# Stationary pieces of a routed-expert layer moved to seven other places in SBUF relative to the weights

## The chip, the cores and the metric

The kernel runs on one core of a Trainium2 chip. The metric is the device time of one execution in microseconds (us). Three executions of the kernel before took 2636.76, 2640.47 and 2642.72 us; the median is 2640.47 us.

The core has a matrix engine (PE in the profile), which takes a stationary operand (128 columns, loaded by LDWEIGHTS, shown as PEld) and streams a moving operand past it (MATMUL); a vector engine (DVE), a scalar engine (ACT), GpSimd (POOL) and SyncE (SP), which issues most of the transfers. SBUF is the on-chip memory: 128 partitions, in each of which a tile takes one range of byte addresses.

## The reference

One transformer-like layer in float32 over 2048 tokens of width 1024. Cut to what the change touches:

```python
y_lru = (h_f + h_b) * gelu(ga)                       # 512 columns, recurrent branch
y_ret = head_rms(o).reshape(B, T, 512) * silu(g)     # 512 columns, retention branch
x = x + g1 * (concatenate([y_lru, y_ret]) @ w_out)   # output projection
h = modulate(rmsnorm(x), sh2, sc2)
s = sigmoid(h @ w_router); eidx, gates = top 6 of 64 experts, by groups
routed = sum over a token's 6 experts of gate * (silu(h @ w1[e]) * (h @ w3[e])) @ w2[e]
x = x + g2 * (routed + shared expert)                # expert width 256
out = rmsnorm(x)
```

## The kernel before, in words

Float32 products run on PE in a reduced format (`F32R`), in three passes: each operand is split into a high part and the low remainder, and a product is high x high, high x low and low x high. The weights are always the moving operand, 512 columns at a time; the activations are the stationary operand, in pieces of 128 columns (512 bytes per partition). Both lie in SBUF. So each MATMUL of a product is preceded by a LDWEIGHTS of a 512-byte piece, and reads 2048 bytes of weights per partition.

The program has four stages, one after the other: `front` (input projection, scans, chunk states), `mixer_out` (retention output, output projection L1745, router, lists of tokens per expert), `experts` (shared expert in 16 blocks of 128 tokens, then 136 blocks of routed tokens, two to a loop turn), and `final` (last norm).

In `mixer_out`, `out_products` (L1745) multiplies four stationary tiles with the output weights: `yl_hi`, `yl_lo`, `y_ret_t_hi`, `y_ret_t_lo`.

In `experts`, `step` on PE does for one block k: 16 matmuls with `x_t[0]` (tile `x_exp_t_hi`; 8 pieces against the high weights and again against the low ones, into `ps_h`), two transposes of the block before (`ps_ht`), 8 matmuls with `x_t[1]` (`x_exp_t_lo`), 8 transposes of the gathered rows for the next block (`ps_x`), and `down` for the block before: for each half of 512 output columns, 4 matmuls with `h_t[0]` (`h_exp_t_hi`) and 2 with `h_t[1]` (`h_exp_t_lo`) into `ps_y`. That is 40 product matmuls and 10 transposes. The helper `products` issues all the product matmuls of this stage at L2429. Blocks alternate between two halves (`par` 0 and 1) of `x_t` and `h_t`. ACT writes the high parts (L2205, L2196, L2211), DVE the low parts (L2261, L2267); ACT (L2182, L2186) and DVE (L2247, L2252) split each expert's weights from the raw ring `w_exp` into the tile called `shared` once per expert, POOL gathers token rows (L2135) and adds the results back to memory (L2145), and SP loads raw expert weights. The order of each engine's work is written out by hand and held together by semaphores; it does not depend on where tiles lie.

Two smaller products of `mixer_out` serve as comparisons below: `ps_o` at L1814 takes the same stationary tile `qf_t` (256 modulo 512) against `sf_ctx` (128 modulo 512) in one `par` and against `sf_m` (256) in the other. Of tiles that transfers read or write, `shared_raw` and `xt` begin at 0 modulo 64, `kvqg_out` and `xa_ga_out` at 32.

Tiles are placed one behind the other in the order in which they are allocated, each rounded up to 32 bytes. In the built program the split weights (the tile `shared`) begin at byte 19200 of every partition, which is 256 modulo 512, and every 512-column block of them is a multiple of 2048 bytes further. Before the change every stationary tile of a product also begins at 256 modulo 512 (`x_exp_t_hi` at 208640, `x_exp_t_lo` at 216832, `h_exp_t_hi` at 225024, `yl_hi` at 188160, `y_ret_t_hi` at 212736), and its pieces lie 512 bytes apart: the distance from stationary to weights is 0 modulo 512 throughout.

Of the kernel before, what the change touches and what calls it, by code (L numbers as in the profile page):

```python
# [19 lines left out]
F32R = mybir.dt.float32r  # L20
# [1389 lines left out]
def mixer_out(nc, for_dma, io, mod_d, hx_d, rec_d, yl_d, h2_d, h2t_d, sum_d, list_d, sf, ident, gc, Z, early, R, pre, pre_loaded):  # L1410
# [4 lines left out]
    with ExitStack() as ctx:  # L1415
        def sb(name, shape, dt=F32):
            return ctx.enter_context(nc.sbuf_tensor(name, shape, dt))
# [17 lines left out]
        rec = Z.rec  # L1435
        x = sb("x_m", [P, 2, D])
        yl_raw = sb("yl_m", [P, 2, NCT * P])
        yl = [sb("yl_hi", [P, 2, NCT * P]), sb("yl_lo", [P, 2, NCT * P])]
        q_t = sb("q_t", [P, HD])
        qf_t = sb("qf_t", [P, HD])  # L1440
        qb_t = sb("qb_t", [P, HD])
# [2 lines left out]
        sfd = sb("sf_decayed", [P, HD])  # L1444
        sq_o = sb("sq_out_o", [P, HEADS, DH])
        y = sb("y_ret", [P, HD])
        y_t = [sb("y_ret_t_hi", [P, HD]), sb("y_ret_t_lo", [P, HD])]
        x1, h2 = Z.x1, Z.h2
        sq_x = sb("sq_out_x", [P, D])
        gain = sq_x  # L1450
# [457 lines left out]
    return out  # L1908


def experts(nc, for_dma, io, mod_d, h2_d, h2t_d, sum_d, list_d, ident, Z, R, pre, pre_loaded, blocks_row, ends_row):

# [8 lines left out]
    N_GU, N_D = WE // CHUNK, WD // CHUNK  # L1921
    STAGES = WE // D
    FIRST_SPLIT = NT - 4
    with ExitStack() as ctx:
        def sb(name, shape, dt=F32):
            return ctx.enter_context(nc.sbuf_tensor(name, shape, dt))
# [10 lines left out]
        w_raw = sb("w_exp", [P, RING * W])  # L1937
        w = Z.w_exp
        g2, gate, who = Z.g2, Z.gate, Z.who.bitcast(U32)
        block_row = sb("block_rows", [P, 2], U32)  # L1940
        take = sb("take", [P, 2], U32)

        lists = R.eq6[:].rearrange("p b j e -> p (b j e)")[:, 0:4 * P].rearrange("p (c t w) -> p c t w", c=2, w=2)
        xg, y = pre[:, 0:2], pre[:, 2:4]
        x_t = [sb("x_exp_t_hi", [P, 2, KC * P]), sb("x_exp_t_lo", [P, 2, KC * P])]
        th, hg = Z.th, Z.hg
        h_t = [sb("h_exp_t_hi", [P, 2, D_EXP]), sb("h_exp_t_lo", [P, 2, D_EXP])]
        nt, nti, end, ones = Z.nt, Z.nti.bitcast(I32), Z.end, Z.ones
# [6 lines left out]
        give = sb("give", [P, 2], U32)  # L1955
        kc = sb("size_key_col", [P, 1])
        ncol = sb("nt_col", [P, 1])
        rnk = sb("size_rank", [P, 1])
        er, de = Z.er, Z.de
        ecol = sb("expert_cols", [P, 2])  # L1960
        bcol = sb("block_cols", [P, 2, 2])
        scol = sb("start_cols", [P, 2])
# [216 lines left out]
        def _(act):  # L2179
# [8 lines left out]
            def copy_shared(k, par):  # L2188
                if k == 0:
                    act.wait_ge(pre_loaded, 32)  # L2190
                else:
                    act.wait_ge(xs_loaded[k % STAGES], (k // STAGES + (k % STAGES > 0)) * 16)
                wait(act, h_done, k - 1)
                for b in range(2):
                    c = slice(b * 512, (b + 1) * 512)
                    act.activation(x_t[0][:, par, c].bitcast(F32R), stage(k)[:, c], ACT.Copy).then_inc(xt_hi, 1)  # L2196

            def copy_xt(k, par):
                if isinstance(k, int) and k < NT:
                    copy_shared(k, par)  # L2200
                    return
                wait(act, h_done, k - 1)
                for b in range(2):
                    act.wait_ge(xt_done, (k - NT) * 2 + 1 + b)
                    act.activation(x_t[0][:, par, b * 512:(b + 1) * 512].bitcast(F32R), ps_x[:, b],  # L2205
                                   ACT.Copy).then_inc(xt_hi, 1)

            def copy_ht(k, par):
# [33 lines left out]
        def _(dve):  # L2242
# [12 lines left out]
            def copy_xt(k, par):  # L2255
                wait(dve, h_done, k - 1)
                for b in range(2):
                    c = slice(b * 512, (b + 1) * 512)
                    dve.wait_ge(xt_hi, k * 2 + 1 + b)
                    src = stage(k)[:, c] if isinstance(k, int) and k < NT else ps_x[:, b]  # L2260
                    dve.tensor_tensor(x_t[1][:, par, c].bitcast(F32R), src, x_t[0][:, par, c],  # L2261
                                      ALU.subtract).then_inc(xt_lo, 1)

            def copy_ht(k, par):
# [51 lines left out]
            def sizes(tabs):  # L2316


                dve.wait_ge(R.carry_done, NT)
                dve.wait_ge(gu_hi, N_GU)  # L2320
                dve.wait_ge(rows_done, 1)
                tabs.of(dve.scalar_tensor_tensor(nt[:, 1:NE], R.iota[:], -float(LIST), R.carry[:], ALU.mult, ALU.add))
                tabs.of(dve.tensor_scalar(nti[:], nt[:, 1:NE], float(P - 1 - LIST), None, ALU.add))
                tabs.of(dve.tensor_scalar(nti[:], nti[:], 7, None, ALU.arith_shift_right))
                tabs.of(dve.tensor_copy(nt[:, 1:NE], nti[:]))
                tabs.of(dve.tensor_scalar(nt[:, 1:NE], nt[:, 1:NE], 1.0, None, ALU.max))
                tabs.of(dve.scalar_tensor_tensor(key[:], nt[:, 1:NE], float(N_EXP), R.iota[:], ALU.mult, ALU.subtract))
# [3 lines left out]
                tabs.of(dve.tensor_reduce(ncol[:], own_key[:], AX.X, ALU.add))
                tabs.of(dve.tensor_scalar(own_key[:], key[:], kc[:], None, ALU.is_gt))
                tabs.of(dve.tensor_reduce(rnk[:], own_key[:], AX.X, ALU.add))
                dve.tensor_scalar(by_size[:, 0], R.rank_at[:], rnk[:], ncol[:], ALU.is_equal, ALU.mult).then_inc(sized, 1)
                dve.tensor_scalar(by_size[:, 1], R.rank_at[:], rnk[:], R.kcol[:, 2:3], ALU.is_equal, ALU.mult).then_inc(sized, 1)
# [80 lines left out]
        def _(pe):  # L2416
# [39 lines left out]
            def step(k, par, r):  # L2456
# [4 lines left out]
                pe.wait_ge(gu_hi, (e + 1) * N_GU)  # L2461
                pe.wait_ge(xt_hi, (k + 1) * 2)
                wait(pe, hg_done, k - 1)
                products(ps_h[:, par], x_t[0][:, par], w[0], at, KC, 512, start=True)
                pe.wait_ge(gu_lo, (e + 1) * N_GU)
                products(ps_h[:, par], x_t[0][:, par], w[1], at, KC, 512)
# [3 lines left out]
                products(ps_h[:, par], x_t[1][:, par], w[0], at, KC, 512, stop=True).then_inc(h_done, 1)  # L2470
# [100 lines left out]
def build(nc, io, out):  # L2571
# [16 lines left out]
    with ExitStack() as for_dma, ExitStack() as ctx:  # L2588
# [6 lines left out]
        early = for_dma.enter_context(nc.semaphore("rec_loaded0"))  # L2595
        front(nc, for_dma, io, mod_d, hx_d, xa_d, ga_d, kr_d, rec_d, yl_d, h2_d, sum_d, list_d, sf, ident, gc, Z, early)
        blocks_row = Z.blocks_row
        ends_row = ctx.enter_context(nc.sbuf_tensor("ends_row", [1, NE + 1], I32))
        with ExitStack() as routing:
            R = Routing(nc, routing, for_dma)  # L2600
            pre = routing.enter_context(nc.sbuf_tensor("w_shared_raw", [P, 4, D], F32))
            pre_loaded = for_dma.enter_context(nc.semaphore("pre_loaded"))
            mixer_out(nc, for_dma, io, mod_d, hx_d, rec_d, yl_d, h2_d, h2t_d, sum_d, list_d, sf, ident, gc, Z, early, R, pre, pre_loaded)
            experts(nc, for_dma, io, mod_d, h2_d, h2t_d, sum_d, list_d, ident, Z, R, pre, pre_loaded, blocks_row, ends_row)
        final(nc, for_dma, io, sum_d, out)


# [14 lines left out]
```

## Time and profile before

| | |
|---|---|
| median of three executions | 2640.47 us (2636.76 to 2642.72) |
| the profiled execution's own time | 2637.47 us |
| its span, first to last instruction | 2635.7 us |
| PE busy | 2461.7 us, 93% of the span |
| PE weight loads busy | 2011.9 us, 76% |
| DVE, ACT, POOL busy | 1717.1, 1012.1, 988.2 us |
| mean granted PE clock | 0.97 of 2.4 GHz |
| product matmuls of `experts` (L2429) | 2432 + 1216 + 1216 + 608 = 5472 of 11959 PE instructions |

The duration of one MATMUL in the profile includes the time for its result to leave the array, which overlaps the next one. What a matmul costs in a dense run is the distance from one start to the next. A merged line of the timeline gives it: the line's length, less the length of one instruction, over the count less one.

### The profile page before, as it was taken

The page shows a single profiled execution, that of the slowest core. Times are in us where ns is not written, and L with a number is a line of the kernel's source. Part 1 is how long each engine was busy: PE and PEld are TensorE (multiplying, and loading weights), DVE is VectorE, ACT ScalarE, POOL GpSimd, SP SyncE. Part 2 cuts the span into 40 slices and gives each one's busy share as a digit, 9 for nine tenths or more (in the row PEclk, how much of TensorE's full clock was granted, in tenths as well). Part 3 has the DMA queues.
Part 4 walks back from the last instruction along what each step waited for, and adds up shares of the span by engine and source line. Part 5 has one row for each costly group of instructions (what it writes and reads, how often), then busy time and mean ns, then how long its engine had stood idle before and what let it go on. Part 6 is the DMA issues. An engine that isn't in the chain of part 4 may idle for free. (4 is left out here: it accounts for less than half of the span.)

```text
span 2635.7 us, 47416 instructions
## 1 busy us (share of the span) xinstructions
PE 2461.7 (93%) x11959; PEld 2011.9 (76%) x11960; DVE 1717.1 (65%) x2741; ACT 1012.1 (38%) x1619; POOL 988.2 (37%) x1009
## 2 busy tenths in 40 slices
PE   7999999998989999889999999999999999999990
PEld 4788777776767888668888887887888888888870
DVE  4663674557345666765567768587876768778673
ACT  2321433333432222222334445354554535445442
POOL 1211016542153677741233333333333433434344
PEclk8999999999989999989999999999999999999995
DMA  7775676756766556346869979899997989979887
GB/s 295 280 284 219 233 274 243 273 210 231 282 240 236 195 188 199 126 133 167 247 169 268 282 209 304 220 301 280 286 315 193 278 256 302 292 215 307 258 239 279
DMA packets 240999, 646.32 MB, mean 245 GB/s; under 512 B 24205, under 2 KB 37841, under 8 KB 224913
## 3 DMA queue, kind: packets, MB, share of 16 engines
q1 hardware_dynamic: 190480, 463.95, 49.1%
q0 software_dynamic: 50432, 181.27, 27.5%
q8 instruction: 48, 0.79, 0.1%
q14 instruction: 39, 0.31, 0.0%
HBM read 467.81 MB, written 177.33 MB: 245 GB/s over the span
## 5 line engine op out<-in xcount | busy, mean ns | idle before, releaser
L2429 PE MATMUL ps_h<-shared,x_exp_t_hi 128*128 (+1 forms) x2432 | 580.0, 391 | 7.4 <-ACT x_exp_t_hi L2196 7.4
L2429 PEld LDWEIGHTS ps_h<-shared,x_exp_t_hi 128*128 128x128 f32 x2432 | 457.2, 188 | 104.5 <-issue 9.1
L2145 POOL DMA_INDIRECT sum_d<-w_shared_raw,give x136 | 236.7, 1740 | 612.1 <-DMA sum_d<-w_shared_raw,give 276.5
L1216 PE MATMUL ps_p<-shared 128*128 128x512 f32 x1632 | 392.5, 399 | 6.5 <-DVE kvqg_out L105 3.3
L1216 PEld LDWEIGHTS ps_p<-shared 128*128 128x128 f32 x1632 | 308.5, 190 | 75.9 <-DVE kvqg_out L105 4.1
L2429 PE MATMUL ps_y<-shared,h_exp_t_hi 128*128 (+1 forms) x1216 | 342.4, 404 | 19.0 <-DVE h_exp_t_lo L2267 14.7
L2429 PE MATMUL ps_h<-shared,x_exp_t_lo 128*128 (+1 forms) x1216 | 318.6, 404 | 0.0
L2247 DVE TENSOR_TENSOR shared<-w_exp,shared (+1 forms) x256 | 307.0, 1220 | 10.0 <-ACT shared L2182 4.7
L2211 ACT ACTIVATE h_exp_t_hi<-ps_ht 128x256 fp32r<-128x256 f32 x152 | 58.4, 384 | 615.5 <-PE ps_ht L2438 613.3
L2429 PEld LDWEIGHTS ps_y<-shared,h_exp_t_hi 128*128 128x128 f32 x1216 | 220.1, 190 | 62.3 <-issue 22.0
L2182 ACT ACTIVATE shared<-w_exp (+1 forms) x256 | 255.4, 1056 | 22.5 <-DMA w_exp<-in_experts 19.5
L2429 PEld LDWEIGHTS ps_h<-shared,x_exp_t_lo 128*128 128x128 f32 x1216 | 216.9, 188 | 39.2
L2289 DVE SCALAR_TENSOR_TENSOR w_shared_raw<-ps_y,shared_raw 128x512 f32<-128x512 f32 x272 | 191.4, 745 | 81.4 <-PE ps_y L2429 59.3
L2429 PE MATMUL ps_y<-shared,h_exp_t_lo 128*128 (+1 forms) x608 | 189.6, 393 | 0.0
L2135 POOL DMA_INDIRECT w_shared_raw<-h_d,take x139 | 147.9, 1064 | 108.8 <-POOL take L2133 105.9
L2261 DVE TENSOR_TENSOR x_exp_t_lo<-ps_x,x_exp_t_hi 128x512 fp32r<-128x512 f32 x274 | 175.6, 682 | 0.0
L2305 DVE SCALAR_TENSOR_TENSOR shared_raw<-shared_raw,ps_h 128x256 f32<-128x256 f32 x152 | 63.8, 420 | 147.8 <-ACT shared_raw L2216 137.9
L2267 DVE TENSOR_TENSOR h_exp_t_lo<-ps_ht,h_exp_t_hi 128x256 fp32r<-128x256 f32 x152 | 64.2, 422 | 141.0 <-ACT h_exp_t_hi L2211 138.2
L2252 DVE TENSOR_TENSOR shared<-w_exp,shared (+1 forms) x130 | 153.1, 1219 | 2.0 <-ACT shared L2186 2.0
L2205 ACT ACTIVATE x_exp_t_hi<-ps_x 128x512 fp32r<-128x512 f32 x274 | 148.1, 594 | 2.2
L2423 PEld LDWEIGHTS ps_x<-ident,w_shared_raw 128*128 128x128 f32 x1096 | 128.1, 141 | 18.6
L2423 PE MATMUL ps_x<-ident,w_shared_raw 128*128 128x128 f32 x1096 | 141.9, 272 | 0.0
(296 smaller groups left out, 3601.8 us busy)
## 6 DMA issues: line engine op xcount, KB each, us to landing
w_exp<-in_experts SPq DMA_DIRECT2D x386, 512.0 KB
shared<-hx_d SPq DMA_DIRECT2D x58, 1024.0 KB, 7.1
shared<-rec_d SPq DMA_DIRECT2D x16, 1536.0 KB
shared_raw<-in_w_mod_rest POOLq DMA_DIRECT2D x16, 1024.0 KB, 5.7
rec_d<-shared_raw SPq DMA_DIRECT2D x48, 256.0 KB, 5.0
rec_d<-kvqg_out SPq DMA_DIRECT2D x48, 256.0 KB, 4.6
hx_d<-shared SPq DMA_DIRECT2D x10, 1024.0 KB, 5.8
xt<-in_xt POOLq DMA_DIRECT2D x18, 512.0 KB, 8.3
```

What stands on the lines that cost most here:

```text
L1216: last = pe.matmul(ps_p[:, s % 2], hx0[:, at, x, k].bitcast(F32R), wa[w][:, k, p % 2 * HD:(p % 2 + 1) * HD].bitcast(F32R), start=(m + k == ...
L2135: pool.indirect_dma_start(xg[:, par], None, h2_d[:, :], bass.IndirectOffsetOnAxis(take[:, par:par + 1], 0)).then_inc(gathered[par], 16)
L2145: pool.indirect_dma_start(sum_d[:, :], bass.IndirectOffsetOnAxis(give[:, par:par + 1], 0), y[:, par], None, compute_op=ALU.add).then_inc(a ...
L2182: act.activation(w[0][:, piece(e, i)].bitcast(F32R), raw(e, i), ACT.Copy).then_inc(gu_hi, 1)
L2205: act.activation(x_t[0][:, par, b * 512:(b + 1) * 512].bitcast(F32R), ps_x[:, b], ACT.Copy).then_inc(xt_hi, 1)
L2247: dve.tensor_tensor(w[1][:, piece(e, i)].bitcast(F32R), raw(e, i), w[0][:, piece(e, i)], ALU.subtract).then_inc(gu_lo, 1)
L2252: dve.tensor_tensor(w[1][:, piece(e, i)].bitcast(F32R), raw(e, i), w[0][:, piece(e, i)], ALU.subtract).then_inc(wd_lo, 1)
L2261: dve.tensor_tensor(x_t[1][:, par, c].bitcast(F32R), src, x_t[0][:, par, c], ALU.subtract).then_inc(xt_lo, 1)
L2267: dve.tensor_tensor(h_t[1][:, par].bitcast(F32R), ps_t[:, 0:D_EXP], h_t[0][:, par], ALU.subtract).then_inc(ht_lo, 1)
L2289: dve.scalar_tensor_tensor(y[:, par, c], ps_y[:, i], gate[:, bass.ds(k, 1)], g2[:, c], ALU.mult, ALU.mult).then_inc(y_done, 1)
L2423: last = pe.transpose(ps_x[:, b, j * P:(j + 1) * P], xg[:, par, c:c + P], ident[:])
L2429: last = pe.matmul(out, x[:, j * P:(j + 1) * P].bitcast(F32R), w_part[:, bass.ds(w_at + j * stride, 512)].bitcast(F32R), start=(start and ...
```

## The change

It moves tiles and changes nothing else: the 10522 instructions of the built program stand in the same order on every engine with the same operations and waits; only addresses differ.

- `experts`: `x_exp_t_hi` and `x_exp_t_lo` are cut into a tile for each `par`, with 128 unused bytes between them. Modulo 512 they begin at 0, 128, 256 and 384. `h_exp_t_hi` and `h_exp_t_lo` begin at 384. Room for this comes from packing the small column tiles into one (`small_cols`) and putting `ends_row` into an idle part of `R.prod`.
- `mixer_out`: unused tiles (`apart_m0` to `apart_m3`) put `yl_hi` at 192 and `yl_lo` at 224 modulo 512; `y_ret_t_hi` begins at 272 and `y_ret_t_lo` at 264.
- Since `ends_row` is gone, everything allocated behind it begins 288 bytes earlier: the raw ring `w_exp` at 159136 instead of 159424 (32 instead of 0 modulo 64), the rows that are gathered and scattered (`w_shared_raw`) at 142752 instead of 143040.

| stationary tile | distance from the weights before | after | matmuls |
|---|---|---|---|
| `x_exp_t_hi`, par 0 | 0 | 256 | 1216 |
| `x_exp_t_hi`, par 1 | 0 | 384 | 1216 |
| `x_exp_t_lo`, par 0 | 0 | 0 | 608 |
| `x_exp_t_lo`, par 1 | 0 | 128 | 608 |
| `h_exp_t_hi` and `_lo` | 0 | 128 | 1216 + 608 |
| `yl_hi` | 0 | 448 | 256 |
| `yl_lo` | 0 | 480 | 128 |
| `y_ret_t_hi` | 0 | 16 | 256 |
| `y_ret_t_lo` | 0 | 8 | 128 |

(distance modulo 512 bytes, stationary less weights)

```diff
@@ mixer_out
-        yl = [sb("yl_hi", [P, 2, NCT * P]), sb("yl_lo", [P, 2, NCT * P])]
+        sb("apart_m0", [P, 56])
+        yl_hi_t = sb("yl_hi", [P, 2, NCT * P])
+        sb("apart_m1", [P, 8])
+        yl = [yl_hi_t, sb("yl_lo", [P, 2, NCT * P])]
...
-        y_t = [sb("y_ret_t_hi", [P, HD]), sb("y_ret_t_lo", [P, HD])]
+        sb("apart_m2", [P, 8])
+        y_t_hi = sb("y_ret_t_hi_at", [P, HD + 4])
+        sb("apart_m3", [P, 120])
+        y_t_lo = sb("y_ret_t_lo_at", [P, HD + 2])
+        y_t = [y_t_hi[:, 4:], y_t_lo[:, 2:]]
@@ experts
+    ENDS_AT = 2 * N_EXP + 2 * NE + 6
...
-        block_row = sb("block_rows", [P, 2], U32)
-        take = sb("take", [P, 2], U32)
+        small = sb("small_cols", [P, 24])
+        block_row, take, give = (small[:, i:i + 2].bitcast(U32) for i in (0, 2, 4))
+        kc, ncol, rnk = (small[:, i:i + 1] for i in (6, 7, 8))
+        ecol, scol = small[:, 9:11], small[:, 11:13]
+        bcol = small[:, 13:17].rearrange("p (c j) -> p c j", c=2)
...
-        x_t = [sb("x_exp_t_hi", [P, 2, KC * P]), sb("x_exp_t_lo", [P, 2, KC * P])]
+        x_t_hi = [sb("x_exp_t_hi0", [P, KC * P])]
+        sb("apart_hi", [P, 32])
+        x_t_hi.append(sb("x_exp_t_hi1", [P, KC * P]))
+        sb("apart_hi_lo", [P, 32])
+        x_t_lo = [sb("x_exp_t_lo0", [P, KC * P])]
+        sb("apart_lo", [P, 32])
+        x_t_lo.append(sb("x_exp_t_lo1", [P, KC * P]))
+        x_t = [x_t_hi, x_t_lo]
...
+        ends_row = R.prod[:].rearrange("p j e -> p (j e)")[0:1, ENDS_AT:ENDS_AT + NE + 1].bitcast(I32)
...
-                products(ps_h[:, par], x_t[0][:, par], w[0], at, KC, 512, start=True)
+                products(ps_h[:, par], x_t[0][par], w[0], at, KC, 512, start=True)
@@ build
-        ends_row = ctx.enter_context(nc.sbuf_tensor("ends_row", [1, NE + 1], I32))
```

## Rows read from the trace of the kernel before

**Rows 1.** The page, busy time of each engine with share and instructions.
```profile
PE 2461.7 (93%) x11959; PEld 2011.9 (76%) x11960; DVE 1717.1 (65%) x2741; ACT 1012.1 (38%) x1619; POOL 988.2 (37%) x1009
```

**Rows 2.** Windows: stretch, its length, busy time of each engine, PE clock, DMA share, GB/s.
```profile
960.00:1150.00 190.00, 160.89 (x933) 138.37 (x932) 132.01 (x423) 50.21 (x139) 131.11 (x131) 0.93 0.49 165
1300.00:1600.00 300.00, 300.00 (x1480) 249.68 (x1479) 206.65 (x299) 126.65 (x200) 107.43 (x128) 1.00 0.83 240
2200.00:2540.00 340.00, 336.76 (x1657) 279.25 (x1656) 260.69 (x362) 168.36 (x252) 133.10 (x144) 1.00 0.93 282
```

**Rows 3.** Waits, 1150 to 2540 us: who waited for whom, us, times, longest.
```profile
PE ps_y L2429 <- DVE h_exp_t_lo L2267: 10.9, 11, 2.2
ACT shared L2182 <- DMA w_exp<-in_experts: 19.5, 14, 3.6
```

**Rows 4.** Timeline of PE, one expert block: start, length (us), instruction, count.
```profile
1503.85 3.79 PE L2429 MATMUL ps_h<-shared,x_exp_t_hi 128*128 x16
1507.48 0.38 PE L2438 MATMUL ps_ht<-ident,shared_raw 128*128 128x128 f32 x2
1507.62 2.10 PE L2429 MATMUL ps_h<-shared,x_exp_t_lo 128*128 x8
1509.56 1.03 PE L2423 MATMUL ps_x<-ident,w_shared_raw 128*128 128x128 f32 x8
1511.82 1.07 PE L2429 MATMUL ps_y<-shared,h_exp_t_hi 128*128 x4
1513.18 2.20 PE L2429 MATMUL ps_h<-shared,x_exp_t_hi 128*128 x9
```

**Rows 5.** Timeline of PE, first five and last six of those sixteen matmuls.
```profile
1503.85 1.30 PE L2429 MATMUL ps_h<-shared,x_exp_t_hi 128*128 x5
...
1506.12 1.53 PE L2429 MATMUL ps_h<-shared,x_exp_t_hi 128*128 x6
```

**Rows 6.** Line L1745, 815 to 836 us: duration ns min/median/max, starts, form.
```profile
L1745 PE MATMUL ps_u<-shared,y_ret_t_hi x16: 389/389/389, 822.5 to 826.8; 128*128 128x512 f32 x16
```

**Rows 7.** Timeline of PE, output projection in the mixer.
```profile
822.49 1.98 PE L1745 MATMUL ps_u<-shared,y_ret_t_hi 128*128 128x512 f32 x8
```

**Rows 8.** The context states' products: timeline, then durations of line L1238.
```profile
494.34 1.89 PE L1238 MATMUL ps_kt_kv<-shared_raw 128*128 128x256 f32 x8
...
L1238 PE MATMUL ps_kt_kv<-shared_raw x8: 377/379/379, 494.3 to 495.9; 128*128 128x256 f32 x8
```

**Rows 9.** Timeline of PE, retention output with either state tile.
```profile
947.69 0.39 PE L1813 MATMUL ps_o<-shared,scores_t 128*128 128x128 f32 x2
947.91 0.39 PE L1814 MATMUL ps_o<-sf_ctx,qf_t 128*128 128x128 f32 x2
948.13 0.39 PE L1815 MATMUL ps_o<-shared,qb_t 128*128 128x128 f32 x2
...
967.78 0.39 PE L1813 MATMUL ps_o<-shared,scores_t 128*128 128x128 f32 x2
968.00 0.39 PE L1814 MATMUL ps_o<-sf_m,qf_t 128*128 128x128 f32 x2
968.23 0.39 PE L1815 MATMUL ps_o<-shared,qb_t 128*128 128x128 f32 x2
```

**Rows 10.** DMA issues: count, KB each, median us from issue to landing.
```profile
rec_d<-shared_raw SPq DMA_DIRECT2D x48, 256.0 KB, 5.0
rec_d<-kvqg_out SPq DMA_DIRECT2D x48, 256.0 KB, 4.6
xa_ga_out<-in_w_mod_head SPq DMA_DIRECT2D x2, 1024.0 KB, 11.1
xt<-in_w_mod_head SPq DMA_DIRECT2D x2, 1024.0 KB, 12.1
```

**Rows 11.** Instruction groups of ACT and DVE: count, busy us, mean ns, idle before.
```profile
L2205 ACT ACTIVATE x_exp_t_hi<-ps_x 128x512 fp32r<-128x512 f32 x274 | 148.1, 594 | 2.2
L2261 DVE TENSOR_TENSOR x_exp_t_lo<-ps_x,x_exp_t_hi 128x512 fp32r<-128x512 f32 x274 | 175.6, 682 | 0.0
```

More of the change, by code:

```diff
@@ L1908, in constants, with experts @@
     return out
-def experts(nc, for_dma, io, mod_d, h2_d, h2t_d, sum_d, list_d, ident, Z, R, pre, pre_loaded, blocks_row, ends_row):
+def experts(nc, for_dma, io, mod_d, h2_d, h2t_d, sum_d, list_d, ident, Z, R, pre, pre_loaded, blocks_row):
     RING = 2
@@ L1954, in experts @@
         cmpe = room[:, 2 * N_EXP:2 * N_EXP + 2 * NE].rearrange("p (c e) -> p c e", c=2)
[L1955 to L1958, printed above, removed]
         er, de = Z.er, Z.de
-        ecol = sb("expert_cols", [P, 2])
-        bcol = sb("block_cols", [P, 2, 2])
-        scol = sb("start_cols", [P, 2])
+        ends_row = R.prod[:].rearrange("p j e -> p (j e)")[0:1, ENDS_AT:ENDS_AT + NE + 1].bitcast(I32)
         ps_h = ctx.enter_context(nc.psum_tensor("ps_h", [P, 2, 512], F32))
@@ L2195, in copy_shared @@
                     c = slice(b * 512, (b + 1) * 512)
-                    act.activation(x_t[0][:, par, c].bitcast(F32R), stage(k)[:, c], ACT.Copy).then_inc(xt_hi, 1)
+                    act.activation(x_t[0][par][:, c].bitcast(F32R), stage(k)[:, c], ACT.Copy).then_inc(xt_hi, 1)
             def copy_xt(k, par):
@@ L2204, in copy_xt @@
                     act.wait_ge(xt_done, (k - NT) * 2 + 1 + b)
-                    act.activation(x_t[0][:, par, b * 512:(b + 1) * 512].bitcast(F32R), ps_x[:, b],
+                    act.activation(x_t[0][par][:, b * 512:(b + 1) * 512].bitcast(F32R), ps_x[:, b],
                                    ACT.Copy).then_inc(xt_hi, 1)
@@ L2260, in copy_xt @@
                     src = stage(k)[:, c] if isinstance(k, int) and k < NT else ps_x[:, b]
-                    dve.tensor_tensor(x_t[1][:, par, c].bitcast(F32R), src, x_t[0][:, par, c],
+                    dve.tensor_tensor(x_t[1][par][:, c].bitcast(F32R), src, x_t[0][par][:, c],
                                       ALU.subtract).then_inc(xt_lo, 1)
@@ L2328, in sizes @@
                 tabs.of(dve.tensor_tensor(own_key[:], key[:], ident[:, 0:N_EXP], ALU.mult))
-                tabs.of(dve.tensor_reduce(kc[:], own_key[:], AX.X, ALU.add))
+                tabs.of(dve.tensor_reduce(kc, own_key[:], AX.X, ALU.add))
                 tabs.of(dve.tensor_tensor(own_key[:], nt[:, 1:NE], ident[:, 0:N_EXP], ALU.mult))
[L2331 to L2335, printed above, removed]
+                tabs.of(dve.tensor_reduce(ncol, own_key[:], AX.X, ALU.add))
+                tabs.of(dve.tensor_scalar(own_key[:], key[:], kc, None, ALU.is_gt))
+                tabs.of(dve.tensor_reduce(rnk, own_key[:], AX.X, ALU.add))
+                dve.tensor_scalar(by_size[:, 0], R.rank_at[:], rnk, ncol, ALU.is_equal, ALU.mult).then_inc(sized, 1)
+                dve.tensor_scalar(by_size[:, 1], R.rank_at[:], rnk, R.kcol[:, 2:3], ALU.is_equal, ALU.mult).then_inc(sized, 1)
             def counts(tabs):
@@ L2463, in step @@
                 wait(pe, hg_done, k - 1)
-                products(ps_h[:, par], x_t[0][:, par], w[0], at, KC, 512, start=True)
+                products(ps_h[:, par], x_t[0][par], w[0], at, KC, 512, start=True)
                 pe.wait_ge(gu_lo, (e + 1) * N_GU)
-                products(ps_h[:, par], x_t[0][:, par], w[1], at, KC, 512)
+                products(ps_h[:, par], x_t[0][par], w[1], at, KC, 512)
                 if not isinstance(k, int) or k > 0:
@@ L2469, in step @@
                 pe.wait_ge(xt_lo, (k + 1) * 2)
-                products(ps_h[:, par], x_t[1][:, par], w[0], at, KC, 512, stop=True).then_inc(h_done, 1)
+                products(ps_h[:, par], x_t[1][par], w[0], at, KC, 512, stop=True).then_inc(h_done, 1)
                 if not isinstance(k, int) or k >= NT - 1:
@@ L2603, in build @@
             mixer_out(nc, for_dma, io, mod_d, hx_d, rec_d, yl_d, h2_d, h2t_d, sum_d, list_d, sf, ident, gc, Z, early, R, pre, pre_loaded)
-            experts(nc, for_dma, io, mod_d, h2_d, h2t_d, sum_d, list_d, ident, Z, R, pre, pre_loaded, blocks_row, ends_row)
+            experts(nc, for_dma, io, mod_d, h2_d, h2t_d, sum_d, list_d, ident, Z, R, pre, pre_loaded, blocks_row)
         final(nc, for_dma, io, sum_d, out)
```

## Prediction, made before the changed kernel was run

> **What bounds the kernel now.** I read the page first: PE is busy 93% of the span, DVE 65%, the others less than half [rows 1]. A share over the whole program hides stages with different limits, so I took the windows next. From 1300 to 1600 us, inside the routed experts, PE is busy 300.0 of 300 us at full clock, and from 2200 to 2540 us 336.8 of 340, while DVE has 206.7 and 260.7 there; only the mixer's second half is looser, 160.9 of 190 [rows 2]. The waits from 1150 to 2540 us agree: the largest wait of PE is 10.9 us in total, and the raw expert weights, which ACT awaits for 19.5 us in all, never appear as what held PE up [rows 3]. So in the experts the time is the sum of the matmul spacings, and a nanosecond more or less on each product matmul comes straight out at the end. The change touches exactly that and nothing else: the order of instructions is the same, so no wait, no transfer and no queue position is added or removed.
>
> **What one product matmul costs now.** One block runs from 1503.85 to 1513.18 us, 9.33 us [rows 4]; 152 blocks of that length are 1418 us. In it, sixteen matmuls with the high part of x take (3.79 - 0.389) / 15 = 0.2267 us each, 0.389 being the length of a single undisturbed one [rows 4, 6]. Transposes take (1.03 - 0.27) / 7 = 0.109 each [rows 4]. The two transposes and the eight low-part matmuls behind them last 1509.56 - 1507.48 = 2.08 us; less 2 x 0.109 that is 1.862 / 8 = 0.2328 us a matmul, so a product run behind transposes is dearer than a clean one, by 6.1 ns each [rows 4]. In the mixer the clean rate is the same, (1.98 - 0.389) / 7 = 0.2273 [rows 6, 7]. And there is a stream without the surcharge: the eight float32 products of the context states take (1.89 - 0.379) / 7 = 0.2159 us each, although a 128 x 128 load stands before each of them too [rows 8]. They stream 256 columns in the time in which a product streams 512, so they read SBUF at half the pace. From 0.2159 to 0.2267 are 10.8 ns a matmul: something about reading 512 columns at the doubled pace beside a load costs that. Whether it depends on where the two operands lie is the whole question.
>
> **The change part by part.** Moved relative to the weights are, by the instruction counts, 2432 matmuls with the high part of x (half to distance 256, half to 384), 608 of the 1216 with the low part (to 128), 1824 with the two parts of h (to 128), and in the mixer 256 (448), 128 (480), 256 (16) and 128 (8): 4864 in the experts and 768 in the mixer, 5632 together. 608 with the low part of x stay at distance 0.
>
> No row of before has a full-pace product at another distance modulo 512, so the cost of the move has to be bounded. Below: at best each moved matmul loses the whole surcharge, -10.8 ns x 5632 = -61 us [rows 4, 8]. Above: the nearest dearer rate is the disturbed one, +6.1 ns x 5632 = +34 us [rows 4]. I take 0, for three reasons.
>
> First, the distance does change within one run today, in larger steps, and nothing happens. Pieces lie 512 bytes apart and their weight blocks 2048, so over the eight pieces the distance passes through 0, 512, 1024 and 1536 modulo 2048. The first five matmuls of the run take (1.30 - 0.389) / 4 = 0.228 and the last six (1.53 - 0.389) / 5 = 0.228 [rows 5]. Even the middle is uniform, or the length of the sixteen would not fit. So no address bit above 512 bytes matters.
>
> Second, arithmetic on the two readers. A load passes 512 bytes of a partition in the 0.109 us that a transpose with its load takes [rows 4], while the stream of 2048 bytes in 0.2267 us passes about 1000. The stream therefore moves at twice the load's pace, and during one load the difference of the two addresses runs once through 512 bytes whatever it was at the start. If memory were divided in banks that repeat within 512 bytes, each load would meet the stream as often from any starting distance, only in another order. This is inference, not a reading, and it does not exclude that the order matters.
>
> Third, the nearest comparison at another distance. The retention output uses stationary `qf_t` with `sf_ctx` at distance 128 and with `sf_m` at distance 0. Two matmuls with either take the same step: 948.13 - 947.91 = 0.22 and 968.23 - 968.00 = 0.23 us [rows 9]. These are float32 and load-bound, so the witness is weak, but it points to nothing.
>
> For the mixer's four places the same value, 0, with 768 x (-10.8 to +6.1 ns) = -8.3 to +4.7 us inside the bounds above. A distance of 8 bytes is the only one that is not a multiple of 16, and it has 128 matmuls: at 6.1 ns 0.8 us.
>
> The Trainium skill has a rule on this: "SBUF — State Buffer", section "Who interferes with whom", gives PE two independent read ports, one for the moving operand and one for the loads, and says that PE never waits on anyone. By that rule place cannot matter and the sum would be 0, as forecast; but this trace disagrees with its plainest reading, since 0.2267 against 0.2159 us is a surcharge that a wholly free second port would not leave [rows 4, 8].
>
> Two side effects. Everything allocated behind the removed `ends_row` starts 288 bytes earlier, which moves the raw weight ring and the gathered rows from 0 to 32 modulo 64. Transfers to and from such tiles exist today: stores of 256 KB land in 5.0 us from a tile at 0 and in 4.6 from one at 32, loads of 1024 KB in 12.1 and 11.1 us [rows 10]. So 0, and the cover that hides a small loss is the 19.5 us that ACT, not PE, waits for these loads [rows 3]. The copies that fill the stationary tiles, 594 ns on ACT and 682 ns on DVE, keep their shapes; even 10% on each of the pair would be 0.13 us per tile half in a block of 9.33 us, hidden while DVE has a quarter of its time free [rows 2, 11]. Packing the small columns changes addresses of single-column operands only: 0.
>
> The sum is 0. Against the profiled execution's 2637.5 us that gives 2637.5; the median of the three executions is 3 us above it, and I forecast against that: 2640 us.
>
> **The rivals.**
> *Slower: some of the new distances collide more.* Runs behind transposes show that a product matmul can cost 0.2328 instead of 0.2267 at distance 0, so the surcharge depends on how load and stream stand to each other in time [rows 4]; a shift in address can act like a shift in time, and my second reason says nothing on order. If all expert places settle at the dearer rate: 6.1 ns x 4864 = +30 us, 2670. If only the most used, distance 128, does (608 + 1824 = 2432 matmuls): +15 us, 2655. It decides from 1 ns on 5632 matmuls, 5.6 us, upward. Against it stand the even rate over eight pieces and the retention pair [rows 5, 9].
> *Faster: the surcharge is a conflict of equal places.* At distance 0 load and stream start in the same residue; a start half a period away might avoid the meeting. All of the experts' matmuls freed: -10.8 x 4864 = -53 us, 2588; only distance 256 freed: 1216 x 10.8 = -13 us, 2627. DVE would still fit (260.7 us of work in 340 - 12 or so) [rows 2]. The skill's "TensorE: Matmul & The Clock Gate", section "Back-to-back issue gap", gives about 216 ns for 512 columns at full clock, which is the price a freed matmul would have; the trace shows it only in the half-pace stream [rows 8]. Against it: the even rate over four distances modulo 2048.
> *Slower by transfers: the ring at 32 modulo 64.* Slower loads would lengthen ACT's waits first and PE's only at the changes of expert. There are 64 of those; an uncovered 0.1 us at each is 6 us, 2646, and that is the point from which it decides. The landings speak against it [rows 10].
>
> **How the numbers follow.** Two medians of this kernel can be told apart at about 0.2%, 5.3 us. No measurable change: 0.60. Slower by address: 0.19; slower by transfers: 0.03. Faster by address: 0.18. The no-change case alone spans 2635 to 2646. The range goes on to 2660 above (the one-place case at 2655 inside, all places at 2670 outside, about 0.07) and to 2622 below (one freed place at 2627 inside, more outside, about 0.09), which leaves out some 0.16 to 0.2. Faster 0.18, same 0.60, slower 0.22.
>
> **What the changed profile would show.** If I am right, the run of sixteen `ps_h` matmuls is 3.79 us long in both halves of the loop, the single matmul 389 ns, and the eight behind the transposes end 2.08 us after the transposes begin, alike with the moved low part (par 1) and the unmoved one (par 0). The low part gives a control inside one trace: if par 1 and par 0 differ, place matters. The mixer's `y_ret_t_hi` run stays 1.98 us. I am wrong if runs of sixteen differ from 3.79 us by more than 0.02 us (1 ns each), or if they are equal and PE instead shows new waits on ACT or DVE at a change of expert.

## The result: 16 us slower, and the profile after

| | before | after |
|---|---|---|
| median (range) of four executions each, us | 2640.29 (2636.76 to 2642.72) | 2656.73 (2654.84 to 2659.96) |
| ratio, with its 95% interval | | 1.0061 [1.0048, 1.0074] |
| span of the profiled execution | 2635.7 | 2655.9 |
| front, up to the mixer | 778.4 | 776.6 |
| mixer | 356.7 | 360.8 |
| shared expert, 16 blocks | 144.9 | 146.7 |
| routed experts, 136 blocks | 1293.2 | 1309.3 |
| final norm | 62.5 | 62.6 |

The stages are worked out from the starts of PE's instructions in the two traces. The experts carry the change, with a smaller part in the mixer. The page's busy line of the changed kernel, beside [rows 1]:

```profile
PE 2478.9 (93%) x11959; PEld 2015.3 (76%) x11960; DVE 1723.3 (65%) x2741; ACT 1011.1 (38%) x1619; POOL 988.7 (37%) x1009
```

PE is busy 17.2 us longer with the same 11959 instructions. The windows of the changed kernel, in the stretches and columns of [rows 2]:

```profile
960.00:1150.00 190.00, 158.50 (x914) 135.48 (x913) 132.07 (x411) 49.84 (x138) 126.20 (x129) 0.93 0.49 162
1300.00:1600.00 300.00, 300.00 (x1465) 247.60 (x1464) 205.59 (x296) 125.33 (x200) 108.26 (x127) 1.00 0.83 236
2200.00:2540.00 340.00, 335.47 (x1625) 276.03 (x1624) 259.73 (x358) 167.29 (x250) 126.92 (x141) 0.99 0.91 274
```

From 1300 to 1600 us PE is as full as before and at the same clock, but gets through 1465 instructions instead of 1480: each takes longer, nothing is waited for. The waits, 1150 to 2560 us, beside [rows 3]:

```profile
ACT shared L2194 <- DMA w_exp<-in_experts: 30.4, 17, 4.0
...
PE ps_y L2441 <- DVE h_exp_t_lo L2279: 14.6, 13, 2.2
```

ACT's wait for raw weights grew by 11 us, and PE's largest by 3.7. PE's belongs to the changes of expert, and what these cost varies from run to run: blocks longer than 9.7 us were 12, with 15.1 us above 9.35 each, before; 13 with 21.6 us after; and 12 with 20.3 us in a kernel below whose time is that of before. I don't count it to the change.

The timeline of PE in one loop turn (two blocks), start, length, instruction, count, answers to [rows 4]. The block at 1500.64 is par 1, the one at 1510.11 par 0:

```profile
1500.64 3.88 PE L2441 MATMUL ps_h<-shared,x_exp_t_hi 128*128 x16
1504.36 0.38 PE L2450 MATMUL ps_ht<-ident,shared_raw 128*128 128x128 f32 x2
1504.50 2.11 PE L2441 MATMUL ps_h<-shared,x_exp_t_lo 128*128 x8
1506.45 1.04 PE L2435 MATMUL ps_x<-ident,w_shared_raw 128*128 128x128 f32 x8
...
1508.71 1.10 PE L2441 MATMUL ps_y<-shared,h_exp_t_hi 128*128 x4
...
1510.11 3.80 PE L2441 MATMUL ps_h<-shared,x_exp_t_hi 128*128 x16
1513.75 0.38 PE L2450 MATMUL ps_ht<-ident,shared_raw 128*128 128x128 f32 x2
1513.88 2.10 PE L2441 MATMUL ps_h<-shared,x_exp_t_lo 128*128 x8
1515.82 1.03 PE L2435 MATMUL ps_x<-ident,w_shared_raw 128*128 128x128 f32 x8
...
1518.08 1.10 PE L2441 MATMUL ps_y<-shared,h_exp_t_hi 128*128 x4
```

One trace holds both the damage and its control. The sixteen matmuls of par 1, at distance 384, last 1504.36 - 1500.64 = 3.72 us up to the transposes; the same sixteen of par 0, at 256, last 1513.75 - 1510.11 = 3.64, which is the 3.63 of [rows 4]. Medians over the 64 turns or so between 1290 and 2520 us, in us; the twelve matmuls of `h` are what is left of a block, less eight transposes at 0.109:

| part of a block | distance after | before | after |
|---|---|---|---|
| sixteen with `x_exp_t_hi`, par 0 | 256 | 3.632 | 3.639 |
| sixteen with `x_exp_t_hi`, par 1 | 384 | 3.632 | 3.724 |
| two transposes and eight with `x_exp_t_lo`, par 0 | 0 | 2.070 | 2.071 |
| the same, par 1 | 128 | 2.070 | 2.087 |
| twelve with `h_exp_t_hi`, `_lo`, either par | 128 | 2.752 | 2.782, 2.786 |
| loop turn | | 18.653 | 18.833 |

The differences of the parts (7 + 92 + 1 + 17 + 30 + 34 = 181 ns) are the turn's 180 ns, and 76 turns of it are 13.7 us, half of them from par 1's sixteen. With the mixer's 4.1 us that is 17.8 us, inside the timed difference of 12.7 to 19.5 us. The two profiled executions are 20.2 us apart; what the turns and the mixer leave of that lies in the changes of expert, some 4 us, and in a front that was 1.8 us shorter.

In the mixer the output projection, beside [rows 7], and the half-pace streams, beside [rows 8, 9]; `qf_t` is now 96 bytes from `sf_ctx` and 0 from `sf_m`:

```profile
819.85 1.98 PE L1752 MATMUL ps_u<-shared,y_ret_t_hi_at 128*128 128x512 f32 x8
...
822.60 2.03 PE L1752 MATMUL ps_u<-shared,y_ret_t_hi_at 128*128 128x512 f32 x8
...
493.96 1.89 PE L1238 MATMUL ps_kt_kv<-shared_raw 128*128 128x256 f32 x8
...
947.22 0.39 PE L1821 MATMUL ps_o<-sf_ctx,qf_t 128*128 128x128 f32 x2
...
967.37 0.39 PE L1821 MATMUL ps_o<-sf_m,qf_t 128*128 128x128 f32 x2
```

The full-pace runs are longer in part. From one start to the next inside a run, the median of 32 runs of each tile went from 226.7 to 232.8 ns for `yl_lo` (distance 480), from 226.7 to 231.7 for `y_ret_t_lo` (8) and from 241.7 to 242.9 for `yl_hi` (448; its runs contain a slow start behind transposes). The runs of `y_ret_t_hi` (16) fall in two groups, both visible above: behind `yl_lo` all but two of 16 stay at 226.7 ns (the 1.98 us line, as before), behind `y_ret_t_lo` all but one of 16 take 233.3 (the 2.03 us line); the other kernel with moved mixer tiles, an experiment below, has the same two groups. The place is the same in both, so at this distance it does not set the rate alone: what ran before the run has a part. By their counts the four tiles make 2.6 us of the stage's 4.1. In the kernels with unmoved mixer tiles the stage took 352.4 to 358.8 us, in both with moved ones 360.8, so the rest is within what a stage varies. The half-pace streams shown don't react.

### The profile page after: what moved, and what is told of

Read it like the earlier page. It is cut to its first block and busy times, and to the rows that moved or that the text cites. A ratio compares the mean times of both kernels' runs of the same rounds, so it can differ in the third digit from the quotient of the medians.

```text
span 2655.9 us, 47416 instructions
## 1 busy us (share of the span) xinstructions
PE 2478.9 (93%) x11959; PEld 2015.3 (76%) x11960; DVE 1723.3 (65%) x2741; ACT 1011.1 (38%) x1619; POOL 988.7 (37%) x1009
## 5 line engine op out<-in xcount | busy, mean ns | idle before, releaser
L2441 PE MATMUL ps_h<-shared,x_exp_t_hi 128*128 (+1 forms) x2432 | 588.3, 394 | 7.4 <-ACT x_exp_t_hi L2208 7.4
L2157 POOL DMA_INDIRECT sum_d<-w_shared_raw,small_cols x136 | 234.2, 1722 | 604.0 <-DMA sum_d<-w_shared_raw,small_cols 282.5
L2147 POOL DMA_INDIRECT w_shared_raw<-h_d,small_cols x139 | 147.9, 1064 | 108.8 <-POOL small_cols L2145 102.0
```

The lines of the kernel that those rows point to most:

```text
L2147: pool.indirect_dma_start(xg[:, par], None, h2_d[:, :], bass.IndirectOffsetOnAxis(take[:, par:par + 1], 0)).then_inc(gathered[par], 16)
L2157: pool.indirect_dma_start(sum_d[:, :], bass.IndirectOffsetOnAxis(give[:, par:par + 1], 0), y[:, par], None, compute_op=ALU.add).then_inc(a ...
L2441: last = pe.matmul(out, x[:, j * P:(j + 1) * P].bitcast(F32R), w_part[:, bass.ds(w_at + j * stride, 512)].bitcast(F32R), start=(start and ...
```

## The experiments

What the changed trace left open: is it the distance between the two operands, and modulo what; or the absolute place; or something that was moved with it (the raw ring at 32 modulo 64, the packed columns, the gathered rows)? And how large is each place's share of the 16 us? "Length of the sixteen" is from their first start to that of the transposes, median of the routed turns. Edits not shown are unused tiles of the size named. Unless it is said, an experiment's mixer has distance 0 or 256. Where a kernel was executed once, its time says little (of the first experiment's ten, one lies 10 us from the median), and the argument rests on the lengths in its trace.

**All stationary tiles at distance 256, everything else as in the changed kernel.**

```diff
-        x_t_hi = [sb("x_exp_t_hi0", [P, KC * P])]
-        sb("apart_hi", [P, 32])
-        ...
+        xh0 = sb("x_exp_t_hi0", [P, 1024])[:, 0:1024]
+        xh1 = sb("x_exp_t_hi1", [P, 1024])[:, 0:1024]
+        ...            # x_exp_t_lo, h_exp_t_* alike, no apart tiles
```

> The changed kernel with its cut tiles, packed columns and earlier weight ring, but every stationary tile of a product at distance 256 from the weights (0 in none), so 0 modulo 256. Theory A (the distance modulo 256 bytes sets the rate; 0 is the cheap one, 128 a dear one): all runs of sixteen ps_h matmuls at 0.2267 us each as in par 0 of the changed kernel, and the time back at 2640 us +- 4. Theory B (distance modulo 512, and 256 only happened to be cheap for one tile): the h and low-part tiles stay dear, 2648 or more. Theory C (the ring at 32 modulo 64 or the packing costs it): stays at 2657.

Measured: 2642.5 us (10 executions) against 2641.72 (19), ratio 0.9998 [0.9982, 1.0014].

```profile
1506.34 3.80 PE L2437 MATMUL ps_h<-shared,x_exp_t_hi 128*128 x16
1509.97 0.38 PE L2446 MATMUL ps_ht<-ident,shared_raw 128*128 128x128 f32 x2
...
1512.83 1.17 PE L2437 MATMUL ps_y<-shared,h_exp_t_hi 128*128 x4
...
1514.29 1.07 PE L2437 MATMUL ps_y<-shared,h_exp_t_hi 128*128 x4
...
1515.65 3.80 PE L2437 MATMUL ps_h<-shared,x_exp_t_hi 128*128 x16
1519.29 0.38 PE L2446 MATMUL ps_ht<-ident,shared_raw 128*128 128x128 f32 x2
```

Both halves are back at 3.63, `ps_y` at 1.07. So 256 is as good as 0, and ring, packing and cut tiles, all still in this kernel, cost nothing that can be measured. Of these two distances, at least, it is the remainder modulo 256 that counts; a second case, h at 128 and at 384, follows below. The twelve matmuls of h even took 2.736 us against 2.752 before.

**Weights and all stationary tiles 96 bytes earlier together: distance 0 kept.** The kernel before without one tile:

```diff
-        ctx.enter_context(nc.sbuf_tensor("to_256_bytes", [P, 24], F32))
```

> The kernel before with the 96 bytes of padding ahead of the weights left out: weights and stationary tiles all begin 96 bytes earlier (160 modulo 512), distance 0 as before; only the identity tile and sf_ctx stay. Theory A (distance decides): 0.2267 us in the runs of sixteen and 2640 us +- 4. Theory D (the absolute place of a tile decides, 256-byte lines or the like): the runs of sixteen go to 0.230 to 0.233 us and the time to 2650 to 2665.

Measured: 2644.07 against 2641.72 us, ratio 1.001 [0.9996, 1.0024].

```profile
1504.54 3.80 PE L2429 MATMUL ps_h<-shared,x_exp_t_hi 128*128 x16
1508.18 0.38 PE L2438 MATMUL ps_ht<-ident,shared_raw 128*128 128x128 f32 x2
```

The sixteen take 3.635 us in both halves, against 3.632 before, so this absolute place is as good as the old one. The twelve of h took 2.768 instead of 2.752 us; in all a turn is 40 ns longer, 3 us a run, which the timing does not resolve. The identity tile stayed where it was, so the transposes' operands did move against each other.

**Weights moved instead of stationary tiles, to distance 64.** As the first experiment, with the tile in front of the weights cut to 8 columns and x at 0 modulo 512.

> The weights (and all else) begin 64 bytes earlier, the experts' stationary tiles stay at 0 modulo 512: distance 64 by moving the weights. Theory A (the distance, whichever operand is moved): the runs of sixteen at 0.2331 us, alternating near 231 and 235 ns, as with the stationary tile moved to 64 in the first scan; time about 2660. Theory D (the absolute place of the stationary tile): 0.2267, since it stands where it stood in the kernel with all distances at 256; time 2642.

Measured (one execution): 2663.43 us.

```profile
1504.39 3.89 PE L2438 MATMUL ps_h<-shared,x_exp_t_hi 128*128 x16
1508.12 0.38 PE L2447 MATMUL ps_ht<-ident,shared_raw 128*128 128x128 f32 x2
```

3.73 us here and in the next experiment, where x was moved to 64 instead: the length follows the difference of the two addresses, whichever operand moves. The expected alternation did not come: here every step takes 233 ns, there 231 and 236 in turn, although the distance is the same.

**Scans of the distance.** Each puts the tiles of the first experiment at other places, two per kernel for the sixteen, by unused tiles or by a start inside the tile, such as

```diff
-        xh0 = sb("x_exp_t_hi0", [P, 1024])[:, 0:1024]
+        xh0 = sb("x_exp_t_hi0", [P, 1026])[:, 2:1026]     # 8 bytes
```

Distances 32 and 64 (low parts 96 and 160, h 192):

> As the kernel with all distances at 256, but the stationary tiles of the experts at distances of 32 (x high, par 0), 64 (x high, par 1), 96 (x low, par 0), 160 (x low, par 1) and 192 (h) modulo 256. Theory A: the runs of sixteen at 32 and 64 come out between 0.2267 and 0.234 us a matmul, each place with its own figure, and no place under 0.2267; time 2650 to 2670. If every place but 0 costs the same (theory A2, only equality helps): both at 0.2325. If a free place exists: one of them at 0.216.

2657.59 us; 3.730 and 3.730 us, each place within the expected span and none under 0.2267. Then 8 and 48 (low parts 96 and 128, h 224):

> As the scan before it, with distances of 8 (x high, par 0), 48 (x high, par 1), 96 (x low, par 0), 128 (x low, par 1) and 224 (h) modulo 256. Theory A with a smooth dependence: 8 bytes costs nearly nothing (0.227), 48 more. Theory A2 (only exact equality is cheap): 8 bytes is as dear as 128, 0.2325. Time 2645 to 2670.

```profile
1510.78 3.86 PE L2440 MATMUL ps_h<-shared,x_exp_t_hi 128*128 x16
1514.48 0.38 PE L2449 MATMUL ps_ht<-ident,shared_raw 128*128 128x128 f32 x2
...
1520.24 3.89 PE L2440 MATMUL ps_h<-shared,x_exp_t_hi 128*128 x16
1523.97 0.38 PE L2449 MATMUL ps_ht<-ident,shared_raw 128*128 128x128 f32 x2
```

2661.16 us; 3.70 and 3.73: the smooth dependence, with 8 bytes nearly free, is out. Then 4 and 96 (h 160):

> As the kernel with all distances at 256, but 4 (x high, par 0), 96 (x high, par 1, and the low part) and 160 (h) modulo 256. The scans so far gave a matmul in the runs of sixteen 226.9 ns at 240, 227.2 at 0, 231.2 at 8, 233.1 at 32, 233.3 at 48 and 64, 232.7 at 128, 229.1 at 192. Theory A with a smooth edge: 4 bytes about 229, 96 about 233. Theory of a sharp edge (any lead of the stationary piece loses the cheap rate): 4 bytes at 231 or more.

```profile
1510.60 3.88 PE L2439 MATMUL ps_h<-shared,x_exp_t_hi 128*128 x16
1514.32 0.38 PE L2448 MATMUL ps_ht<-ident,shared_raw 128*128 128x128 f32 x2
```

2663.73 us; 3.72 and 3.74: a single float off costs nearly the full price. From the other side, 192 and 240:

> As the kernel with all distances at 256, but x high at 192 (par 0) and 240 (par 1) modulo 256, the rest at 0. Theory A: own figure each; 192 near 0.229 as the h tiles at 192 settled to in the first scan, 240 (16 bytes short of equal) about 0.230. If the dear places are only those ahead of the weights (1 to 128) and not those behind, both at 0.2267 and the time 2642; otherwise 2645 to 2652.

```profile
1505.04 3.83 PE L2439 MATMUL ps_h<-shared,x_exp_t_hi 128*128 x16
1508.70 0.38 PE L2448 MATMUL ps_ht<-ident,shared_raw 128*128 128x128 f32 x2
...
1514.39 3.79 PE L2439 MATMUL ps_h<-shared,x_exp_t_hi 128*128 x16
1518.02 0.38 PE L2448 MATMUL ps_ht<-ident,shared_raw 128*128 128x128 f32 x2
```

2646.18 us; 3.66 and, at 240, 3.63: a second cheap place, where 0.230 a matmul was expected. 184 and 216 (low part of par 0 at 248):

> As the kernel with all distances at 256, but x high at 184 (par 0) and 216 (par 1), x low of par 0 at 248 modulo 256, the rest at 0. Theory A: 184 and 216 between 0.229 and 0.2335 us, 248 like 0 (2.07 us with the two transposes). If a place cheaper than 0 exists in the quarter behind the weights, one of the two is under 0.2265.

```profile
1517.25 3.80 PE L2438 MATMUL ps_h<-shared,x_exp_t_hi 128*128 x16
1520.88 0.38 PE L2447 MATMUL ps_ht<-ident,shared_raw 128*128 128x128 f32 x2
```

2649.69 us; 3.713 and, at 216, 3.635, where at least 0.229 a matmul was expected. The low part at 248 missed too: 2.086 us with its two transposes, not the 2.07 of distance 0. Is 208 to 240 a band? 208 and 224:

> As the kernel with all distances at 256, but x high at 208 (par 0) and 224 (par 1) modulo 256. So far 216, 240 and 0 held 227 ns a matmul and 184 (232) and 192 (229) did not. Theory of a cheap band from somewhere above 192 up to 0: both at 227, 224 included, and the dear h tiles at 224 in the second scan came from the transposes ahead of them. Theory of scattered cheap places: 224 at 233 here too.

```profile
1503.82 3.87 PE L2439 MATMUL ps_h<-shared,x_exp_t_hi 128*128 x16
1507.53 0.38 PE L2448 MATMUL ps_ht<-ident,shared_raw 128*128 128x128 f32 x2
...
1510.40 1.17 PE L2439 MATMUL ps_y<-shared,h_exp_t_hi 128*128 x4
...
1513.24 3.89 PE L2439 MATMUL ps_h<-shared,x_exp_t_hi 128*128 x16
1516.97 0.38 PE L2448 MATMUL ps_ht<-ident,shared_raw 128*128 128x128 f32 x2
```

2650.97 us; 3.71 and 3.73: no band, since both are dear and 216, 240 beside them are cheap.

The same trace shows an effect on tiles that were not moved. From the start of `ps_y` to that of the next sixteen are 1513.24 - 1510.40 = 2.84 us here and 1515.65 - 1512.83 = 2.82 in the first experiment, and `h` and the gathered rows lie where they lay there. As medians the twelve of par 0 take 2.761 against 2.736 us; with x at 240 (par 1) they take 2.754, with x at 216 2.742. So a change of x's place costs up to 25 ns a block in matmuls whose own tiles did not move.

All of it, as length of the sixteen over 16, in ns:

| distance modulo 256 | 0 | 4 | 8 | 32 | 48 | 64 | 96 | 128 | 184 | 192 | 208 | 216 | 224 | 240 |
|---|---|---|---|---|---|---|---|---|---|---|---|---|---|---|
| ns a matmul | 227.0 | 232.3 | 231.2 | 233.1 | 233.3 | 233.1 | 234.0 | 232.8 | 232.1 | 229.1 | 232.1 | 227.2 | 233.2 | 226.9 |

Each figure is that of a run in this order of work. The runs of `y_ret_t_hi` at 16, which take 226.7 or 233.3 ns by what precedes them, warn against carrying a single figure elsewhere.

**All expert tiles at distance 128**, the place that the change used most.

```diff
+        sb("apart_xh0", [P, 32])
         xh0 = sb("x_exp_t_hi0", [P, 1024])[:, 0:1024]
```

> As the kernel with all distances at 256, but all six stationary tiles of the experts at distance 128 modulo 256 (mixer at 0). Theory A (distance modulo 256): both halves' runs of sixteen at 0.2325 us as in par 1 of the changed kernel (+5.7 ns x 2432 = +14 us), the low-part matmuls +2 ns x 1216 (+2.4), the h matmuls about +2.8 ns x 1824 (+5): 2641.5 + 21 = about 2663 us. Theory of neighbours (a tile is dear because its neighbour in time is at another distance): the runs of sixteen fall back to 0.227 and the time to 2645.

Measured: 2659.32 us (4 executions) against 2643.88 (15), ratio 1.0056 [1.004, 1.0071], +14.8 us.

```profile
1503.14 3.88 PE L2438 MATMUL ps_h<-shared,x_exp_t_hi 128*128 x16
1506.86 0.38 PE L2447 MATMUL ps_ht<-ident,shared_raw 128*128 128x128 f32 x2
...
1512.61 3.88 PE L2438 MATMUL ps_h<-shared,x_exp_t_hi 128*128 x16
1516.33 0.38 PE L2447 MATMUL ps_ht<-ident,shared_raw 128*128 128x128 f32 x2
```

3.72 in both halves. The turn is 18.933 us against 18.653 before, and 76 turns of 0.28 would be 21 us; the timed interval ends at 18.8. So the place is confirmed and the size missed: the medians show less than the trace's turns add up to. In the profiled execution the two expert stages together took 20.0 us more than in the first experiment's. That execution, with 2654.61 us the lowest of the four, had a front stage of 773.6 us, against 775.6 to 781.6 in all the other traces, with nothing edited there; but that is one execution, and what the others gave back stays open.

**Only h moved: to 128, and to 224** (`sb("apart_hh", [P, 32])`, `[P, 56]` ahead of it in the first experiment).

> As the kernel with all distances at 256, with h_exp_t_hi and h_exp_t_lo alone at 128 modulo 256. Theory A: the twelve ps_y matmuls of a block take 2.78 instead of 2.74 us, the runs of sixteen stay at 3.63 to 3.64 us: +48 ns x 152 blocks = +7 us, about 2649. Theory G (the parts act on each other, and x and h must both be displaced to cost): no change, 2642.

Measured: 2647.45 us (12) against 2640.84 (18), ratio 1.0025 [1.0013, 1.0038], +6.6 us; turn 18.733.

```profile
1507.98 3.80 PE L2438 MATMUL ps_h<-shared,x_exp_t_hi 128*128 x16
...
1515.95 1.10 PE L2438 MATMUL ps_y<-shared,h_exp_t_hi 128*128 x4
```

The merged line of the sixteen stays at 3.80, `ps_y` goes to 1.10 from 1.07: the term of h alone. The twelve take 2.785 us, as in par 1 of the changed kernel (2.786), although h lies at 128 modulo 512 from the weights there and at 384 here: again only the remainder modulo 256 counts. The sixteen, unmoved, take 3.639 instead of 3.635.

> As the kernel with all distances at 256, with the h tiles alone at 224 modulo 256, behind x tiles at 0. Theory that the transposes ahead decide (a run behind them does not find the cheap rate unless the distance is 0): the twelve ps_y matmuls at 2.80 us, as in the second scan. Theory that the displaced x tiles did it: 2.74 us. Time 2651 or 2642.

2650.9 us (one execution); the twelve take 2.802 us, and took 2.809 and 2.812 at 224 with the x tiles moved too. The displaced x tiles were not what made h dear; as the scans show, what runs before adds some ns of its own.

**The changed kernel with `x_exp_t_hi` par 1 put back to 256.**

```diff
-        sb("apart_hi", [P, 32])
-        x_t_hi.append(sb("x_exp_t_hi1", [P, KC * P]))
+        xh1 = sb("x_exp_t_hi1", [P, 1024])[:, 0:1024]     # right behind par 0
```

> The changed kernel with only x_exp_t_hi of par 1 put from distance 384 to 256 (mixer, h and the low part stay moved). Theory A: its run of sixteen falls from 3.72 to 3.64 us in every second block, 76 x 0.085 = -6.5 us against the changed kernel: about 2650. Theory G: no change against it, 2657.

Measured: 2651.02 us (7) against 2640.84, ratio 1.0042 [1.0024, 1.006]: 11 us above before, where the changed kernel is 16 above.

```profile
1511.60 3.80 PE L2442 MATMUL ps_h<-shared,x_exp_t_hi 128*128 x16
...
1519.57 1.10 PE L2442 MATMUL ps_y<-shared,h_exp_t_hi 128*128 x4
...
1520.97 3.80 PE L2442 MATMUL ps_h<-shared,x_exp_t_hi 128*128 x16
```

Par 1's sixteen are at 3.64 again and the rest stays, but for 5 ns in the low part behind them: 5 us come back of the 6.5 that its 86 ns in each of 76 turns are worth. The two intervals overlap, so the timing alone would not prove it; with the lengths it does.

**The transposes' own operands at distance 0** (`ident` and the gathered rows against the weights), to see whether the dear matmuls behind transposes come from there.

```diff
+        ctx.enter_context(nc.sbuf_tensor("ahead_of_ident", [P, 32], F32))
...
+            routing.enter_context(nc.sbuf_tensor("ahead_of_rows", [P, 24], F32))
```

> All product distances 0 modulo 256, and the identity tile and the rows that are transposed (gathered rows and gated h) at 0 modulo 256 from each other and from the weights too, where they were at 32 to 160. Theory E (the slow first six matmuls behind transposes, 225 to 236 ns, come from the transposes' own distance): those runs settle at once to 0.2267, 8 low-part matmuls 2.03 instead of 2.07 us with their transposes and the h part 2.72 instead of 2.74 to 2.75: -60 ns in each of 152 blocks, -9 us, about 2632. Theory F (they come from the change of pace between the half-pace transposes and the full-pace products, whatever the place): unchanged, 2641 us +- 4.

Measured: 2643.25 us (11) against 2643.88 (15), ratio 0.9996 [0.9987, 1.0005].

```profile
1507.92 0.38 PE L2446 MATMUL ps_ht<-ident,shared_raw 128*128 128x128 f32 x2
...
1509.99 1.04 PE L2431 MATMUL ps_x<-ident,w_shared_raw 128*128 128x128 f32 x8
```

Still 2.07 us from the one to the other, near the 2.08 of [rows 4]: the dear start does not come from there. The twelve of h took 2.749 us in one half and 2.736 in the other, with all distances 0 in both. No version of these beat the kernel before by more than the noise.

## Why the prediction was wrong

What bounds the kernel was read rightly: nanoseconds on a matmul came straight out at the end. The forecast of no change failed at one term, the cost of the moved matmuls, which I put at 0 between the bounds and which the traces show at 13.7 us in the experts and about 2.6 in the mixer.

- **The step that failed is the second reason**, the arithmetic on the two readers: from any start, each load meets the stream equally often, so place cannot matter. I noted that it does not exclude that the order matters, and then took 0 all the same. The place does matter: a matmul of the sixteen costs 227 ns at 0, 216 and 240, and from 229.1 to 234.0 at eleven others.
- **The first reason** was right and said less than I took from it. An even rate over pieces 512 bytes apart shows that no bit above 512 counts; the runs add that 256 doesn't either [rows 5]. It says nothing of 128, where three of the five expert places went.
- **The third reason** was no witness. `qf_t` at 128 and at 0 cost the same, and at 96 and 0 they still do: a median step of 112 ns with either state tile, in both traces [rows 9]. I had called it weak, and let it count.
- **The bounds** held for the sum, but the upper one was no bound on a place. 384 cost +5.8 ns a matmul, under the +6.1 taken from the runs behind transposes [rows 4]; 48 and 96 cost +6.3 and +7.0 in the scans. The +6.1 was itself no steady rate: behind the two transposes the steps are 317, 224, 231, 236, 228, 233, 231 ns, a slow start averaged over eight. Below, nothing came near -10.8 ns: the lowest is 226.9.
- **The rival "slower by address" was right in its mechanism**, and the two rates of `y_ret_t_hi` at one distance bear out its thought that place and order in time act together, and its one-place case came to 2655 us against 2656.7 measured, but by another sum. It gave 6.1 ns to the 2432 matmuls at 128. Measured: 1216 at 384, which is 128 modulo 256, at 5.8 ns (7.0 us, left out there); h's 1824 at a net 2.6 ns (4.8 us); 608 low parts at 2.1 ns (1.3 us); 256 free (0.5 us); and the mixer 4.1 us, which lies inside the +4.7 bound that I gave it. A run behind transposes is already dear at distance 0, and place added less there; why is not shown.
- **"Faster by address"** fell: half a period away, at 128, is dearer, and 256 bytes are no distance at all. The Trainium skill ("SBUF — State Buffer", section "Who interferes with whom") gives PE two independent read ports and has it wait for nobody. The runs disagree: the same load and stream take 227 or 234 ns a matmul when nothing but tiles' addresses differs. Here I weighed a trace's 10.8 ns surcharge against that rule and still let the rule's result, 0, stand.
- **Side effects at 0** were right: the first experiment has them all, at a ratio of 0.9998. One effect hid inside: the twelve `ps_y` matmuls are 16 ns a block cheaper in that experiment (2.752 to 2.736 us). Against it h's move costs about 48 ns, not 32, so a third of it is masked in the changed kernel. Which of the moves did that is not shown: the gathered rows lie 288 bytes earlier there, but with the rows in that same place other x tiles bring the twelve to 2.754 and 2.761.
- **The announced control** did its work: the low parts of par 1 and par 0 differ by 17 ns, and the sixteen differ from 3.79 us by more than 0.02.

## What to carry to other kernels

Where PE bounds a kernel with full-pace 512-column products and a load ahead of each, put each stationary tile and the weights that it meets at the same address modulo 256 bytes, which was cheap in every kernel that had it; one float off already costs 5 ns of 227. Read it from the length of a merged run in the timeline and compare runs that differ in place only: 0.09 us in 3.6 is plain there and hard to see in two medians. When a term of a sum has bounds from both sides and the only reason for its middle is an argument that says itself what it leaves open, look for the rows that would bear on just that, or give the bound more weight.

## What the runs showed of the hardware that was not expected

- The cost of a product matmul depends on the difference of its operands' addresses modulo 256 bytes, whichever moves. The cheap places found, 0, 216 and 240, are scattered; 208 and 224 between them are dear (227 against 232 and 233 ns).
- It depends on what ran before, too: at distance 16, runs of eight hold 226.7 ns behind one tile's run and 233.3 behind another's, in the same trace.
- The spacings inside a run repeat: at 0 each is 227 ns; at 128 they go, on average, 232, 239, 232, 231, 232, 229, 231 and begin again; at 192 they go 229, 232, 226. A likely reading is that each load's meeting with the stream sets when the next pair starts, and that 0 is a place which leads back to itself. The two rates at distance 16 fit this. That is argued, not shown.
- No steady run went below 226.6 ns a step, while the half-pace stream takes 215.9 [rows 8]. What the remaining 11 ns are stays open, as does why, behind transposes, from two to nine steps after the first take 224 to 240 ns even at distance 0.
- With h at distance 0 modulo 256 the twelve matmuls behind the transposes take from 2.736 to 2.768 us (first and second experiment), by the places of other tiles. Which tile does it is not separated.
